# Chunk inverses of a gated scan on 32x32 diagonal blocks: four quadrants of the array for the first five levels

## What is computed

```python
def step(state, inp):
    r_t, w_t, k_t, v_t, a_t, b_t = inp
    sa = jnp.einsum('bhvk,bhk->bhv', state, a_t)
    state = (state * w_t[:, :, None, :] + sa[..., :, None] * b_t[:, :, None, :]
             + v_t[..., :, None] * k_t[:, :, None, :])
    y = jnp.einsum('bhvk,bhk->bhv', state, r_t)
    return state, y
```

## Time and profile before

| | us |
|---|---|
| median of 3 runs (4323.70 to 4324.11) | 4323.84 |
| span of the profiled execution (first to last instruction) | 4318.4 |
| PE busy | 3826.8 (89%) |
| PEld busy | 2369.0 (55%) |
| DVE busy | 1960.7 (45%) |
| ACT busy | 1532.5 (35%) |
| POOL busy | 990.1 (23%) |
| mean granted TensorE clock | 0.949 of full speed |

### The profile page before, as it was taken

One profiled execution on the slowest core, in us unless ns is written; L12 is line 12 of the kernel. 1 busy time (PEld: TensorE's weight loads), 2 busy tenths in 40 slices (PEclk: granted clock), 3 DMA queues, 4 the chain that ended last, 5 costly groups with the idle time before them and its releaser, 6 DMA issues.

```text
span 4318.4 us, 66900 instructions
## 1 busy us (share of the span) xinstructions
PE 3826.8 (89%) x29209; PEld 2369.0 (55%) x29532; DVE 1960.7 (45%) x2105; ACT 1532.5 (35%) x1877; POOL 990.1 (23%) x438
## 2 busy tenths in 40 slices
PE   6988989999999999998899888988889887988787
PEld 3555666666666665446544455555554455555454
DVE  3456454655544554341323356254552256254552
ACT  4222223232332312231213242454463332454462
POOL 2413223332323332131153200111102200111102
PEclk9999999999999999999999988999999988999999
DMA  2111111111111113233220200100002100100002
GB/s 96 54 37 45 36 45 48 48 50 46 51 41 50 46 60 120 109 126 118 109 91 30 96 15 11 35 25 20 30 18 103 44 15 11 35 25 20 30 24 89
DMA packets 61587, 226.96 MB, mean 53 GB/s; under 512 B 6832, under 2 KB 8560, under 8 KB 60784
## 3 DMA queue, kind: packets, MB, share of 16 engines
q1 hardware_dynamic: 52224, 189.64, 12.8%
q10 hardware_dynamic: 9072, 33.03, 1.9%
HBM read 174.93 MB, written 47.71 MB: 52 GB/s over the span
## 4 chain that ended last, share of the span: by engine, by line
PE 68%; DVE 16%; ACT 10%; POOL 2%; issue 2%; DMA 2%; ACTq 0%; DVEq 0%; SPq 0%; POOLq 0%
PE psum L1000 66%; DVE arena L2076 7%; ACT arena L1572 6%; DVE arena L2079 4%; DVE arena L2534 2%; ACT L1572 2%; PE psum L1003 2%; DVE arena L2468 2%; ACT wh L1572 1%; POOL arena L2593 1%; DMA arena<-in_w_proj_conv 1%; POOL hl L2593 1%; POOL wl L2593 1%; ACT arena L2012 0%; DVE arena L2083 0%
## 5 line engine op out<-in xcount | busy, mean ns | idle before, releaser
L1000 PE MATMUL psum<-arena 64*64 64x32 f32 (+12 forms) x18860 | 1451.9, 276 | 261.2 <-DVE arena L2076 93.7
L1000 PEld LDWEIGHTS psum<-arena 64*64 64x64 f32 (+6 forms) x18860 | 1046.0, 157 | 697.4 <-issue 383.0
L2593 POOL TENSOR_TENSOR wl<-arena,wh 128x1024 bf16<-128x1024 f32 (+1 forms) x203 | 491.7, 2422 | 2261.5 <-ACT wh L1572 2258.5
L1000 PE MATMUL psum<-hh,wh 128*128 128x512 f32 x3248 | 916.5, 425 | 94.2 <-ACT hh L1572 27.4
L1572 ACT ACTIVATE arena<-psum 128x512 f32<-128x512 f32 (+4 forms) x660 | 415.8, 630 | 1114.4 <-PE psum L1000 819.7
L1000 PE MATMUL psum<-hh,wl 128*128 128x512 bf16 (+1 forms) x3034 | 777.7, 393 | 24.1 <-issue 10.1
L1000 PEld LDWEIGHTS psum<-hh,wh 128*128 128x128 f32 x3248 | 611.9, 195 | 298.5 <-issue 50.3
L1000 PE MATMUL psum<-hl,wh 128*128 128x512 bf16 x3139 | 752.1, 383 | 20.9 <-issue 9.8
L2076 DVE TENSOR_TENSOR arena<-psum,arena 128x512 f32<-128x512 f32 (+3 forms) x488 | 319.4, 654 | 910.4 <-PE psum L1000 592.6
L2079 DVE SCALAR_TENSOR_TENSOR arena<-arena 128x1024 f32<-128x1024 f32 x356 | 564.7, 1586 | 187.4 <-ACT arena L1572 171.2
L2593 POOL TENSOR_TENSOR arena<-arena 128x1024 f32<-128x1024 f32 (+4 forms) x142 | 364.0, 2563 | 889.1 <-ACT arena L1572 480.5
(11 more groups left out here) (38 smaller groups left out, 822.7 us busy)
## 6 DMA issues: line engine op xcount, KB each, us to landing
arena<-in_w_in SPq DMA_DIRECT2D x161, 512.0 KB, 3.5
scr_g<-arena ACTq DMA_DIRECT2D x24, 512.0 KB, 2.6
arena<-scr_g SPq DMA_DIRECT2D x24, 512.0 KB, 4.5
arena<-in_w_out SPq DMA_DIRECT2D x24, 512.0 KB, 3.5
arena<-in_w_mem_kv SPq DMA_DIRECT2D x16, 512.0 KB, 3.5
scr_x<-arena SPq DMA_DIRECT2D x16, 512.0 KB, 3.6
arena<-scr_x SPq DMA_DIRECT2D x16, 512.0 KB, 7.1
arena<-in_x SPq DMA_DIRECT2D x8, 512.0 KB, 10.7
```

What stands on the lines that cost most here:

```text
L1000: return pe.e.matmul(o, l, r, start=start, stop=stop)
L2593: return pool.seq.tensor_tensor(o, a, b, op)
```

## The change

Levels 0 to 4 never leave the 32x32 blocks on a chunk's diagonal. They are now kept alone: `XD`, `XTD` and `YD` (128x512) hold the two diagonal blocks of a head's 64x64 matrix, one on each 32 partitions. A solve of these levels is 16 chunks x 4 quadrants (`q`) = 64 matmuls with 32 rows and 32 columns of weights that stream 16 columns, into 256 columns of the bank. Level 5 needs only the lower left block: `lower_left` runs 32 matmuls of 32 rows and 32 columns of weights that stream 32 columns. Its product goes through `YL`, copied out by ACT (partitions 32 to 63) and DVE (96 to 127). A new step `whole`, after level 4, spreads XTD over the full XT (ACT the left halves, with a scale of one or zero per partition; POOL the right halves), and `sqe` of level 5 copies the last block into XT (ACT partitions 0 to 31, DVE 64 to 95). `tu` waits for these. Masks, identity and the steps on DVE and POOL shrink to the same 512 columns or 256 elements.

```diff
+    XD, XTD = X[:, 0:512], X[:, 512:1024]
+    YD, YL = Y[:, 0:512], cols3(Y[:, 512:1024], NCH)
...
             do("sqe", ct, lv)
+            if lv == 4:
+                do("whole", ct)
             yield
...
             o, m = bank((name, ct, lv)), 1 << lv
             for n in range(NCH):
+                for q in range(4):
+                    p = slice(32 * q, 32 * q + 32)
+                    x = mm(o[p, 16 * n:16 * n + 16].rearrange("p (b m) -> p b m", m=m), l(p, n, q), r(p, n))
+            x.then_inc(*pe.up(name, ct, lv))
+
+        def lower_left(name, ct, to, l, r):
+
+            o = bank((name, ct, 5))
+            for n in range(NCH):
                 for h in range(2):
-                    p = slice(64 * h, 64 * h + 64)
-                    x = mm(o[p, 32 * n:32 * n + 32].rearrange("p (b m) -> p b m", m=m), l(p, n, h), r(p, n))
-            x.then_inc(*pe.up(name, ct, lv))
+                    p, q = (slice(64 * h + a, 64 * h + a + 32) for a in (32 - to, to))
+                    x = mm(o[q, 32 * n:32 * n + 32], l(p, n, h), r(p, n))
+            x.then_inc(*pe.up(name, ct, 5))
 
         def sx(ct, lv):
             cleared(("sx", ct, lv))
             pe.wait_ge(*at("Gm", ct, 3, 1))
             pe.wait_ge(*(at("X", ct, lv - 1) if lv else at("eye", ct)))
-            solve("sx", ct, lv, lambda p, n, h: G[p, n, h, 0:64], lambda p, n: half(ch(X)[p, n], 0, 1 << lv))
+            if lv == 5:
+                lower_left("sx", ct, 32, lambda p, n, h: G[p, n, h, 32:64], lambda p, n: ch(XD)[p, n])
+            else:
+                solve("sx", ct, lv, lambda p, n, q: G[p, n, q // 2, 32 * (q % 2):32 * (q % 2) + 32],
+                      lambda p, n: half(ch(XD)[p, n], 0, 1 << lv))
...
         def sq(ct, lv):
             cleared(("sq", ct, lv))
+            if lv == 5:
+                pe.wait_ge(*at("YL", ct, 0))
+                pe.wait_ge(*at("YL", ct, 1))
+                pe.wait_ge(*at("XT", ct, 4))
+                return lower_left("sq", ct, 0, lambda p, n, h: YL[p, n], lambda p, n: ch(XTD)[p, n])
...
-            pe.wait_ge(*at("XT", ct, 5))
+            pe.wait_ge(*at("whole_l", ct))
+            pe.wait_ge(*at("whole_q", ct, 0))
+            pe.wait_ge(*at("whole_q", ct, 1))
...
+        def sxe(ct, lv):
+            if lv == 5:
+                act.wait_ge(*at("sx", ct, 5))
+                f(YL[32:64], cols3(bank(("sx", ct, 5)), NCH)[32:64], AF.Copy).then_inc(*act.up("YL", ct, 0))
+
+        def whole(ct):
+            act.wait_ge(*at("XT", ct, 4))
+            if ct:
+                act.wait_ge(*at("tu", ct - 1, 3))
+            f(ch(XT)[:, :, 0:32], ch(XTD), AF.Copy, scale=upper).then_inc(*act.up("whole_l", ct))
+
+        def sqe(ct, lv):
+            if lv == 5:
+                act.wait_ge(*at("sq", ct, 5))
+                act.wait_ge(*at("whole_r", ct))
+                f(ch(XT)[0:32, :, 32:64], cols3(bank(("sq", ct, 5)), NCH)[0:32], AF.Copy).then_inc(*act.up("whole_q", ct, 0))
...
+            if lv == 5:
+                dve.wait_ge(*at("sx", ct, 5))
+                cp(YL[96:128], cols3(bank(use), NCH)[96:128]).then_inc(*dve.up("YL", ct, 1))
...
+            if lv == 5:
+                use = ("sq", ct, 5)
+                dve.wait_ge(*at("whole_r", ct))
+                cp(ch(XT)[64:96, :, 32:64], cols3(bank(use), NCH)[64:96]).then_inc(*dve.up("whole_q", ct, 1))
...
-            tt(half(XT, 1, m), bank(use).rearrange("p (b m) -> p b m", m=m), half(XT, 1, m), ADD).then_inc(*dve.up("XT", ct, lv))
+            tt(half(XTD, 1, m), bank(use)[:, 0:256].rearrange("p (b m) -> p b m", m=m), half(XTD, 1, m), ADD).then_inc(*dve.up("XT", ct, lv))
...
-            pool.seq.memset(Y, 0.0).then_inc(*pool.up("Yz", ct, lv))
+            pool.seq.memset(YD, 0.0).then_inc(*pool.up("Yz", ct, lv))
+
+        def whole(ct):
+            pool.wait_ge(*at("XT", ct, 4))
+            if ct:
+                pool.wait_ge(*at("tu", ct - 1, 3))
+            pool.seq.tensor_copy(ch(XT)[:, :, 32:64], ch(XTD)).then_inc(*pool.up("whole_r", ct))
```

More of the change, by code:

```diff
@@ L220, in build @@
     id64 = cst[:, C_ID64:C_ID64 + 64]
-    ymt = cst[:, C_YT:C_YT + 32]
-    ymask = [cst[:, C_YM + 64 * i:C_YM + 64 * i + 64] for i in range(6)]
+    id32 = cst[:, C_ID32:C_ID32 + 32]
+    upper = cst[:, C_UP:C_UP + 1]
+    ymt = cst[:, C_YT:C_YT + 16]
+    ymask = [cst[:, C_YM + 32 * i:C_YM + 32 * i + 32] for i in range(5)]
     rst = cst[:, C_RST:C_RST + 1024]
@@ L936, in build @@
             ("keys", "init shift lo_tanh ksq ksum kn kn2 lora_load lora lsig cs kh rkh bsum powers bon ar bk"),
-            ("solve", "G eye prep vt ta sx sxe sp sq sqe bt"), ("chain", "decay w0 tu mr dd y0 ch ys"), ("groups", "gmean gsub gvar gnorm gaff gout"),
+            ("solve", "G eye prep vt ta sx sxe sp sq sqe whole bt"), ("chain", "decay w0 tu mr dd y0 ch ys"), ("groups", "gmean gsub gvar gnorm gaff gout"),
             ("side", "glu_s glu spill tap"), ("merge", "back_o back_u fetch merge uadd usum umean usq uvar usqs urs umul uact usil ugate"),
@@ L2640, in sx @@
         def sx(ct, lv):
+            if lv == 5:
+                return
             if lv > 1:
@@ L2657, in sxe @@
                 return
-            x_ = half(XT, 1, 1).rearrange("p (n b) m -> p n (b m)", n=NCH)
+            x_ = half(XTD, 1, 1).rearrange("p (n b) m -> p n (b m)", n=NCH)
             pool.wait_ge(*at("Gm", ct, 3, 1))
[L2660 to L2664, removed]
+            for q in range(4):
+                r = slice(32 * q, 32 * q + 32)
+                gq = G[r, :, q // 2, 32 * (q % 2):32 * (q % 2) + 32].rearrange("p n (b two) -> p n b two", two=2)[:, :, :, 1]
+                tt(x_[r], gq, ymt.unsqueeze(1).to_broadcast([128, NCH, 16])[r], MUL).then_inc(*pool.up("XT00", ct, q))
+            iq = id32.rearrange("p (b two) -> p b two", two=2)[:, :, 1].unsqueeze(1).to_broadcast([128, NCH, 16])
             tt(x_, x_, iq, ADD).then_inc(*pool.up("XT0", ct))
@@ L2876, in constants @@
     c1[:, C_ID64:C_ID64 + 64] = s == t
[L2877 removed]
+    c1[:, C_UP] = p % 64 < 32
+    s, t = p[:, None] % 32, np.arange(32)[None]
+    c1[:, C_ID32:C_ID32 + 32] = s == t
+    for i in range(5):
         m = 1 << i
[L2879 to L2880 removed]
+        c1[:, C_YM + 32 * i:C_YM + 32 * i + 32] = (s // (2 * m) == t // (2 * m)) & ((s // m) % 2 == 1) & ((t // m) % 2 == 0)
+    c1[:, C_YT:C_YT + 16] = s == 2 * np.arange(16)[None]
     c1[:, C_RST:C_RST + 1024] = (np.arange(1024) % CB != 0)[None]
```

42 lines of the change are left out of this document (23 added, 19 removed).

## The result

The changed kernel takes 4368.4 us (median of 4 runs, 4362.44 to 4372.15) against 4323.98 of the kernel before beside it (4 runs, 4323.7 to 4336.67): ratio 1.0092, 95% interval 1.0078 to 1.0107. Forecast were 4242 us and a range from 4207 to 4320. The profiled execution spans 4370.4 us, 52.0 more than before.

A forecast was written before the change was run, and what follows sets the result against it. PE was taken as the bound in the solving stage. -105 (solves) +15 (waits) +8 (instruction fetch) = -82 us, from a span of 4318.4 to 4236.4, forecast as 4242 us of time; range 4207 to 4320.

The forecast's parts named there:

- The pace of a solve: Solving stage, PE: weight loading sets the pace; levels 0 to 4 go from 1.87 to 0.99 us a solve.
- -105: Solving stage: us taken off PE by 120 solves at 0.88 us each; at the bounds 117 and 98.
- the instruction fetch: Pairs of solves on PE: two packets take 2.4 us against 1.98; +8 us taken, 13 unbuffered, none with buffering.
- rival C: Four-quadrant bursts, above all the second half: queue not refilled fast enough, 20.3 ns a record gives +62, near 4386; chance 0.13.
- the clock of 0.98: Solving stage: PE's mean clock, left out of the sum, so no us were given for it.
- Waits that grow: PE's waits in the solving stage for chain work beside shorter solves: 12 us, other solves 3, together +15 us.
- The costs set at nothing: New copies on ACT and POOL and DVE's level-5 evictions: counted as 0; 36 us if the cover were gone.
- The cover named there: Level 5: 5.8 us of PE projections between its two solves and 12.9 us before the reader hide the new copies.
- A: Four-quadrant solves: issue holds them at 14.0 ns a record, 1.79 us a solve; result -22, near 4302; chance 0.17.
- B: Solves: records hold a quadrant 58 ns, or only two row groups work at once; 4323 to 4324; chance 0.09.
- The floor of some 25 ns: Skill's rule for small matmuls, cited against the change: a four-quadrant solve takes 3.2 us, the sum ends near +125.
- What would have shown it: Profile signs: 128-record bursts of about 1.2 us; if wrong, DVE or ACT waits and stage idle from 87 to over 110 us.

The follow-up runs named there:

- the long burst: Kernel before plus two bursts of 512 constant matmuls, one on four 32x32 quadrants (meant here), one on two 64x64: 4384.88 us.
- experiment three: Kernel before with sq also waiting for GpSimd clears between sp and sq of each pair: six clears 4558.71 us, one clear 4447.72 us.
- the last order: Changed kernel with a projection piece in each of a level's three gaps, next tile's two pieces kept apart: 4246.35 us, ratio 0.9806.

## Why the prediction was wrong, step by step

**The pace of a solve held.** Forecast were 31 ns for four quadrants, bounds 28 and 33; it is 4 x 8.5 = 34, just outside, and 2 x 16 = 32 for two quadrants at level 5. A single solve was to be a burst of about 1.2 us, and is one of 1.26. That agrees with the reading that loading weights set the old pace; the rows of the weights were halved together with the columns, so no run shows that the columns alone did it. Instead of -105 the term is about -97.

**The term that failed is the instruction fetch, +8 us with bounds 0 and 13.** It took from the earlier trace rows how long a packet travels, 1.2 us, and set two of these, 2.4 us, against the pair's 1.98: 0.4 us short. But what PE lives on is how far apart blocks arrive, and that is 3.75 us in the long burst. A pair uses two blocks' worth in 2 us, and at the block's end that falls into its second half the next one isn't there: 2.0 us on average, not 0.4, and 36 times. Right was the volume (+52 packets forecast, +53 measured), wrong the price of a packet. The row at hand did not hold that price, and the bounds should have said so: the interval between blocks was bounded by nothing, since the densest long stretch of before, the pair of 128 records, is one block. With "no faster supply known than a record in 29.2 ns" as the upper bound, which is where rival C stood, the term would have reached well past +100.

**A term was missing: the clock.** The working set the clock of 0.98 aside as given. It is a result of how PE is fed. The stops are paid again afterwards, up to +77 us here, about as much as the stops themselves. In experiment three 70.1 us of stops cost 121: a stop is paid 1.7 times.

**Waits that grow, +15: wrong sign.** PE's waits for DVE fell from 45.7 to 33.3 us. Of the seven over 3 us six stayed (the longest 7.6 against 8.0 us), of the fifteen shorter ones four. Why is not shown: the evictions became shorter, and PE's stops gave DVE time, but the last order has the waits as low (35.3 us in 12) with hardly a stop. The costs set at nothing, on ACT and POOL, were nothing: ACT's wait is 20.0 us in 8, as in the earlier trace rows. The cover named there (a projection piece between the level-5 solves) was real.

**The rivals.** *A* and *B* are out by the single burst: 1.26 us, not 2.0 or 2.1. *C* had the side, the band ("above 4332"), the place (the second half of a burst) and the cause ("its queue isn't refilled at that rate") right, at a chance of 0.13, but its form and its price wrong. There is no slow pace inside a burst: records come every 8.5 ns until a block ends whose successor isn't there, and then none for some 2 us. So of the 40 single solves two suffer (0.4 and 1.1 us), of the 32 pairs thirty; at C's cheapest 20.3 ns each of the 104 solves would have lost, to 4386 and more. The floor of some 25 ns that the Trainium skill gives ("TensorE: Matmul & The Clock Gate", Back-to-back issue gap) had the right sign for another reason: the trace disagrees with it, at 8.5 ns a record.

**What would have shown it** named the waits for DVE and the stage's idle time as the loss to look for. The idle time did grow (180 to 1620 us had 87, 180 to 1640 has 130), but under "issue", which that list had not named.

## What to carry to other kernels

Before cutting matmuls into more and smaller ones, count TensorE's instructions, loads included, along its own time: here a dense burst ran freely for 250 to 512 of them, by where in a block it began, and 256 every 3.75 us could be sustained. Where the supply is that close, dense bursts belong between long matmuls and not beside one another; the same quadrants cost 44 us packed together and gained 71 spread out. A stop on the bounding engine is priced with the clock that it loses afterwards, and an edit to the order is tried on the old kernel too, so that one knows which of the two made the difference.

## What was not expected of the hardware

- Four 32x32 quadrants take a record every 8.5 ns, and where no block's end stopped them they kept that up for 256 records, 512 instructions; two at level 5 take one every 16 ns.
- Long bursts of either form, 1024 records with their loads, take 30.1 us. The steady supply of 256 instructions in 3.75 us is just the old quadrants' demand, which is why no stop shows before.
- A stop next to a solve lowers the clock by one level in about as many places whichever quadrants run and whatever causes it: 41 falls with 36 stops under issue, 35 with 32 waits for GpSimd's one clear, 11 where nine stops are left. In the run with one clear 13 falls came behind waits of 0.6 us or less beside a solve; how short a stop can be was not tried.
- Left open: whether a block's 3.75 us is the travel of one request or a rate, that is whether more than one can be under way. In the case shown the packet began 0.2 us before PE stopped (211.67 against 211.87 us) and landed at 213.13, and PE went on at 214.56. No run here asked for a block earlier.
